# Ten weight low parts and five h low parts per FFN move from GpSimd to VectorE, and ScalarE's queue is reordered around them

## The chip, the cores and the metric

The kernel runs on one core of a Trainium2 chip. The metric is the device time of one execution in microseconds. Five engines work side by side, each on its own queue of instructions in program order: TensorE (PE, matmul), VectorE (DVE), ScalarE (ACT), GpSimd (POOL) and SyncE (SP), which issues the DMA transfers. They meet only at semaphores.

## The reference, cut to what matters

Two layers of a decoder trunk, on 544 token columns (512 of a prompt and 32 of samples). Each layer has three residual updates, of which the first and the third are FFNs, and the change touches only them. So there are four FFNs in the program:

```python
def swiglu(x, w_gate, w_up, w_down):
    return (jax.nn.silu(x @ w_gate) * (x @ w_up)) @ w_down

x = x + 0.5 * rmsnorm(swiglu(rmsnorm(x, g[0]), ffn1_w_gate, ffn1_w_up, ffn1_w_down), g[1])
# then the token mixer, then the same with ffn2_* and g[4], g[5]
```

D_MODEL is 1024 (8 chunks of 128) and D_FF 2688 (21 tiles of 128). h = silu(gate) * up is a tensor of 21 tiles of 128 x 544. All values are float32.

## The kernel before, in words

**High and low parts.** The matmuls take operands rounded to a shorter float format (fp32r). To keep the accuracy of float32, each operand is split: `hi` is the rounded value, and `lo = value - hi`. A product of two operands is three matmuls: w_hi with x_hi, w_hi with x_lo, w_lo with x_hi (`pe_step`, L995). ScalarE makes the high parts (`act_high`, L1619 to 1626, a Copy into fp32r), and another engine the low parts by a subtraction.

**Weight blocks.** A block is 128 x 512, four chunks of one weight column tile, so a gate or an up tile takes two blocks. Blocks pass through three rings: `w_raw` with 3 slots (the DMA's target), `w_hi` and `w_lo` with 6 slots each. SyncE may load block n once block n-3 has its low part (`w_split`, L588). ScalarE may make the high part of item n once TensorE has used item n-6 (L1625).

**The up stage of an FFN.** Tiles 0 to 5 (PLAIN_TILES = 6) are plain: 6 gate and 6 up tiles make 12 units of two blocks, blocks 0 to 23. The first three units are done in the opening (`pe_opening`), interleaved with the end of the sublayer before; units 3 to 11 follow in the loop of L1118. Even units are gate tiles, odd units up tiles, and unit i writes the PSUM pair i % 3, so it must wait until VectorE has read unit i-3 from there: an even unit waits for the `up` of two tiles before (`up_read`, L1123), an odd unit for the `gate` of the tile before (`gate_scaled`, L1125). Unit 9, for one, waits for gate(3). Each block also waits for its low part (L1101). The tiles 6 to 20 are then computed as 15 pair steps of seven products each (`pe_product`), with mixed operands that VectorE and ScalarE prepare during units 3 to 11: `x_mix(c)` and `x_lows(c)` for c = 0 to 3 on VectorE, `act_x_operands(c)` on ScalarE. Product `MIXED2`, the third of a step, waits until ScalarE has copied the first product out (`z_kept`, L1149), and for that copy ScalarE waits at the first step for the low part of h tile 4 (L1868).

**Who does what there.** VectorE: `gate(t)` (one operation), `up(t)` (two), `x_mix(c)` (five), `x_lows(c)` (four), then `w_mix` and `w_lower` for the pair steps, in the order of L2488 to 2515. ScalarE: `silu(t)`, `h_high(t)` (the high part of h tile t), `high(i)` and `act_x_operands(c)`, in the order of L1889 to 1919. GpSimd: the low part of every plain weight block (`split`, L877 to 883, the instruction is L882) and of every h tile (`low(t)`, L894 to 898), in the order of L900 to 912. gate(t) for t from 3 on overwrites a buffer that holds h tile t-3, and so waits for that tile's low part (L2377).

The order of all this is written out by hand; there is no planner. SyncE issues the loads in the order of L609 to 643, with the stores of x to a scratch tensor (`x_aside`) and the loads for pair step 0 between the block loads.

Of the kernel before, what the change touches and what calls it, by code (L numbers as in the profile page):

```python
# [18 lines left out]
def program(nc, I, O):  # L19
# [28 lines left out]

    PLAIN_TILES = 6
    LENT_TILES = 4  # L50
    PAIRS = FC - PLAIN_TILES
    UP_PLAIN = 4 * PLAIN_TILES
    PRODUCTS = 7
# [37 lines left out]
    def split_by(n):  # L91

        return plain(n) + 1
# [57 lines left out]
    with ExitStack() as ctx:  # L151
# [166 lines left out]
        def h_tile(t):  # L318

            if t < EARLY_H:  # L320
                return h_hi[:, t, :], h_lo[:, t, :]
            return xn_hi[:, t - EARLY_H, :], xn_lo[:, t - EARLY_H, :]
# [549 lines left out]
        def pool_layer(pool, l, steps):  # L872
# [12 lines left out]
            def splits(i0, i1):  # L885
                for i in range(i0, i1):
                    split(i)

            def up(which):

                f0 = FC * (2 * l + which)
                n_up = (B_UP1, B_UP2)[which]

                def low(t):  # L894
                    hi, lo = h_tile(t)
                    buf = t % 3 if t < PLAIN_TILES else (t - PLAIN_TILES) % 2
                    pool.wait_ge(h_hi_ready, f0 + t + 1)
                    pool.tensor_tensor(lo, gs[:, buf, :], hi.bitcast(F32), ALU.subtract).then_inc(h_ready, 1)  # L898

                splits(n_up, n_up + 14)  # L900
                low(0)
                low(1)
                splits(n_up + 14, n_up + 17)
                low(2)
                splits(n_up + 17, n_up + 21)
                low(3)
                splits(n_up + 21, n_up + UP_PLAIN)
                low(4)
                for t in range(PLAIN_TILES - 1, FC - 1):
                    low(t)  # L910
                splits(n_up + UP_ITEMS, n_up + UP_ITEMS + RING)
                low(FC - 1)

# [729 lines left out]
            act.wait_ge(w_used, n - RING + 1)  # L1643
            act.activation(w_hi[:, n % RING, :], w_sum(w, k, plain(n_up + UP_ITEMS)), ACT.Copy).then_inc(w_hi_ready, 1)

        def act_x_operands(act, l, which, c):

            done = 2 * l + which
            b = c % 2
            act.wait_ge(x_normed, 8 * done + 2 * c + 2)  # L1650
            act.activation(x_first[:, c, 0:HT], stage[:, b, 0, :], ACT.Copy).then_inc(x_op_hi, 1)
            act.activation(x_ops[:, 0:2, c, 0:HT], stage[:, b, 2:4, :], ACT.Copy).then_inc(x_op_hi, 1)
            act.wait_ge(x_mixed, 12 * done + 3 * c + 1)
            act.activation(x_ops[:, 2:4, c, 0:HT], x_ops_f[:, 2:4, c, HT:T], ACT.Copy).then_inc(x_op_hi, 1)
            act.wait_ge(x_mixed, 12 * done + 3 * c + 3)
            act.activation(x_r[:, c:DC:4, 0:HT], x[:, c:DC:4, half(1)], ACT.Copy).then_inc(x_op_hi, 1)
# [165 lines left out]
        def act_ffn(act, l, which):  # L1822

            v = 3 * l + 2 * which
            f0 = FC * (2 * l + which)
            n_up = l * BLOCKS + (B_UP1, B_UP2)[which]
            n_dn = l * BLOCKS + (B_DN1, B_DN2)[which]
            g0 = PLAIN_TILES * (2 * l + which)
            pairs0 = PAIRS * (2 * l + which)

            def silu(t):
                act.wait_ge(gate_scaled, g0 + t + 1)
                act.activation(gs[:, t % 3, :], gs[:, t % 3, :], ACT.Silu).then_inc(silu_done, 1)

            def h_high(t):
                if which == 1 and t == 0:
                    act.wait_ge(cs_stored, 16 * HC * (l + 1))
                act.wait_ge(h_scaled, f0 + t + 1)
                buf = t % 3 if t < PLAIN_TILES else (t - PLAIN_TILES) % 2
                act.activation(h_tile(t)[0], gs[:, buf, :], ACT.Copy).then_inc(h_hi_ready, 1)  # L1840

            def high(i):
                if i < UP_PLAIN:
                    act_high(act, n_up + i)
                elif i < UP_ITEMS:
                    act_high_of_pair(act, l, which, *divmod(i - UP_PLAIN, PRODUCTS))
                else:
                    act_high(act, n_dn + i - UP_ITEMS)

            def second_silu(w):  # L1850
                act.wait_ge(w_used, n_up + UP_PLAIN + PRODUCTS * w + A22 + 1)
                act.activation(gs[:, w % 2, half(1)], ps[:, ZS[w % 2], 0:HT], ACT.Silu).then_inc(silu_kept, 1)

            def pair_step(w):

                n = n_up + UP_PLAIN + PRODUCTS * w
                i = UP_PLAIN + PRODUCTS * w
                mixed = (rstd[:], gs[:, 2, :])[w % 2]
                z = ps[:, ZS[w % 2], 0:HT]

                def keep(k, out, src):
                    act.wait_ge(w_used, n + k + 1)
                    act.activation(out, src, ACT.Copy).then_inc(z_kept, 1)  # L1863

                if w:
                    second_silu(w - 1)
                high(i + 5)
                act.wait_ge(h_ready, f0 + PLAIN_TILES + w - 1)  # L1868
                keep(A11, gs[:, w % 2, half(0)], z)
                high(i + 6)  # L1870
                h_high(PLAIN_TILES + w - 1)
                if w:
                    act.wait_ge(second_summed, 2 * (pairs0 + w) - 1)
                keep(A22MINUS21, p_kept[:], ps[:, SECOND_COLS[w % 2], 0:HT])
                high(i + 7)
                if w == 0:
                    act.wait_ge(h_scaled, f0 + PLAIN_TILES)
                elif w == 1:
                    act.wait_ge(h_ready, f0 + PLAIN_TILES)
                keep(MIXED2, mixed[:, half(0)], z)  # L1880
                high(i + 8)
                high(i + 9)
                keep(A11MINUS21, mixed[:, half(1)], z)
                act.wait_ge(first_summed, pairs0 + w + 1)
                act.activation(gs[:, w % 2, half(0)], gs[:, w % 2, half(0)], ACT.Silu).then_inc(silu_kept, 1)
                high(i + 10)
                high(i + 11)

            act_open(act, v, n_up, [gs[:, 0, :], gs[:, 2, :], gs[:, 1, :]])  # L1889
            silu(0)  # L1890
            silu(1)
            act_x_operands(act, l, which, 0)
            h_high(0)
            h_high(1)
            high(14)
            silu(2)
            high(15)
            act_x_operands(act, l, which, 1)
            high(16)
            h_high(2)  # L1900
            high(17)
            act_x_operands(act, l, which, 2)
            high(18)
            silu(3)
            high(19)
            high(20)
            h_high(3)
            high(21)
            act_x_operands(act, l, which, 3)
            high(22)  # L1910
            silu(4)
            high(23)
            high(24)
            h_high(4)
            high(25)
            high(26)
            silu(5)
            high(27)
            high(28)
            for w in range(PAIRS):  # L1920
                pair_step(w)
            second_silu(PAIRS - 1)
            high(UP_ITEMS + 5)
            h_high(FC - 1)
            act.preload_act_table_set("natural_log_exp_and_others")
            for t in range(DC - 1):
                for b in range(DOWN_BLOCKS):
                    act_high(act, n_dn + DOWN_BLOCKS * (t + 1) + b)
                act_square(act, v, t)
            act_turn_from_ffn(act, v, n_dn + DOWN_BLOCKS * DC)  # L1930
# [422 lines left out]
        def dve_ffn(dve, l, which):  # L2353
# [94 lines left out]
            def w_mix_second(w, n, slot, mixed0):  # L2448
# [8 lines left out]
                dve.wait_ge(w_mixed, mixed0 + 3)  # L2457
                dve.tensor_tensor(slot[6], slot[2], slot[3], ALU.add).then_inc(w_mixed, 1)

            def w_lower(w, k):  # L2460
                n = n_up + UP_PLAIN + PRODUCTS * w + k
                slot = w_slot(w, k, after)
                dve.wait_ge(w_hi_ready, n + 1)
                dve.tensor_tensor(slot, w_sum(w, k, after), w_hi[:, n % RING, :].bitcast(F32), ALU.subtract).then_inc(w_low, 1)  # L2464
# [24 lines left out]
            gate(0)  # L2489
            gate(1)  # L2490
            x_mix(0)
            up(0)
            up(1)
            x_lows(0)
            gate(2)
            x_mix(1)
            up(2)
            x_lows(1)
            x_mix(2)
            gate(3)  # L2500
            x_lows(2)
            up(3)
            x_mix(3)
            gate(4)
            x_lows(3)
            w_mix(0, (0,))
            up(4)
            w_mix(0, (1,))
            w_lower(0, 0)
            w_lower(0, 1)  # L2510
            w_lower(0, 2)
            gate(5)
            w_lower(0, 3)
            w_lower(0, 4)
# [592 lines left out]
```

## Time and profile before

| | us |
|---|---|
| median of 3 runs | 2137.16 |
| lowest and highest | 2136.04, 2138.46 |
| the profiled execution | 2134.72 |
| its span in the trace | 2133.0 |
| TensorE busy in the span | 2096.6 (98%) |
| VectorE busy | 1343.7 (63%) |
| ScalarE busy | 1000.9 (47%) |
| GpSimd busy | 789.9 (37%) |

Read the waits of TensorE first, then the stretch in which they lie, engine by engine. In a timeline a row is one instruction or a run of equal ones: start, duration, engine, line of the kernel, what it writes and reads, how many, and in brackets how long the engine stood idle before it and who ended that. A matmul's duration is modelled and overlaps the next one's, so the pitch of matmuls is read from the starts.

### The profile page before, as it was taken

Reading aid. Unit: us, or ns where it says so; the run is one execution under the profiler, and the core shown is the slowest. Engines: PE = TensorE matmul, PEld = TensorE weight load, DVE = VectorE, ACT = ScalarE, POOL = GpSimd, SP = SyncE. Lnnn points to the kernel's source line nnn. Section 1 sums busy time; section 2 is a strip of 40 time slices with the busy share of each in tenths; the row PEclk is TensorE's granted clock in tenths of the full one; section 3 lists DMA queues with packets and bytes.
Section 4 is the critical chain, followed back from the end, with each engine's and each line's share of the span. In section 5 each row is a group of like instructions: output and inputs, shape, how many; then the busy total and the mean of one; then the engine's idle time right before and its main releaser. Section 6 shows DMA issues by size and latency. Waiting matters only on the chain.

```text
span 2133.0 us, 45510 instructions
## 1 busy us (share of the span) xinstructions
PE 2096.6 (98%) x18864; PEld 2044.2 (96%) x18864; DVE 1343.7 (63%) x2147; ACT 1000.9 (47%) x2031; POOL 789.9 (37%) x645
## 2 busy tenths in 40 slices
PE   8999999999999999999999999999999999999999
PEld 8899999999889989999999999999998899999998
DVE  6999611666457899950189994036554678999313
ACT  5466522534344646652265664235143545566422
POOL 4411374533324431134443113544332354311442
PEclk9999999999999999999999999999999999999999
DMA  5333442322233423343242334333224134233432
GB/s 174 89 100 100 128 110 84 91 71 66 61 93 103 127 85 100 102 128 97 80 138 84 103 100 140 94 89 81 72 61 101 57 114 128 86 103 101 129 90 78
DMA packets 395245, 209.79 MB, mean 98 GB/s; under 512 B 31920, under 2 KB 385472, under 8 KB 395040
## 3 DMA queue, kind: packets, MB, share of 16 engines
q1 hardware_dynamic: 394896, 206.84, 34.3%
q8 instruction: 149, 2.44, 0.5%
q14 instruction: 56, 0.46, 0.1%
q10 hardware_dynamic: 144, 0.06, 0.0%
HBM read 189.18 MB, written 17.67 MB: 97 GB/s over the span
## 4 chain that ended last, share of the span: by engine, by line
PE 83%; DVE 12%; ACT 2%; issue 1%; DMA 1%; POOL 1%; SPq 0%; DVEq 0%; ACTq 0%
PE ps L1001 47%; PE ps L1013 28%; PE ps L1284 1%; DVE x_ops L2420 1%; DVE stage L2399 1%; DVE xn_lo L2222 1%; DVE x_ops L2417 1%; DVE x_ops_f L2402 1%; POOL w_lo L882 1%; DMA w_raw<-in_ffn_w_up 1%; DVE numer L2846 1%; DVE x_r L2422 1%; DVE x L2238 1%; DVE spare L2464 1%; DVE x_first L2415 1%
## 5 line engine op out<-in xcount | busy, mean ns | idle before, releaser
L882 POOL TENSOR_TENSOR w_lo<-w_raw,w_hi 128x512 fp32r<-128x512 f32 (+1 forms) x440 | 578.6, 1325 | 769.2 <-ACT w_hi L1626 767.7
L1001 PE MATMUL ps<-xn_hi,w_hi 128*128 128x272 f32 x2496 | 572.0, 296 | 17.8 <-POOL w_lo L882 13.3
L1001 PE MATMUL ps<-xn_hi,w_lo 128*128 128x272 f32 x2496 | 555.3, 289 | 0.0
L1001 PE MATMUL ps<-xn_lo,w_hi 128*128 128x272 f32 x2496 | 554.2, 289 | 0.0
L1626 ACT ACTIVATE w_hi<-w_raw 128x512 fp32r<-128x512 f32 (+1 forms) x440 | 264.6, 605 | 597.2 <-PE ps L1001 463.0
L1001 PEld LDWEIGHTS ps<-xn_hi,w_hi 128*128 128x128 f32 x2496 | 408.1, 190 | 40.1 <-issue 30.8
L1001 PEld LDWEIGHTS ps<-xn_lo,w_hi 128*128 128x128 f32 x2496 | 409.0, 190 | 0.3
L1001 PEld LDWEIGHTS ps<-xn_hi,w_lo 128*128 128x128 f32 x2496 | 407.1, 190 | 0.0
L1013 PE MATMUL ps<-x_ops,w_hi 128*128 128x272 f32 x1920 | 368.8, 289 | 0.3
L1013 PEld LDWEIGHTS ps<-x_ops,w_hi 128*128 128x128 f32 x1920 | 302.1, 189 | 1.6 <-ACT rstd L1863 1.1
L2204 DVE TENSOR_TENSOR acc<-acc,gs 128x544 f32<-128x544 f32 (+1 forms) x45 | 35.2, 781 | 319.9 <-ACT gs L1696 319.3
L898 POOL TENSOR_TENSOR h_lo<-gs,h_hi 128x544 fp32r<-128x544 f32 x52 | 90.2, 1737 | 299.9 <-ACT h_hi L1840 299.9
L1013 PE MATMUL ps<-x_r,w_hi 128*128 128x272 f32 x960 | 185.6, 288 | 2.2 <-ACT gs L1863 2.2
L1001 PE MATMUL ps<-h_hi,w_hi 128*128 128x272 f32 x832 | 181.1, 289 | 0.0
L1001 PE MATMUL ps<-h_lo,w_hi 128*128 128x272 f32 x832 | 180.3, 288 | 0.0
L1001 PE MATMUL ps<-h_hi,w_lo 128*128 128x272 f32 x832 | 180.2, 288 | 0.0
L1013 PEld LDWEIGHTS ps<-x_r,w_hi 128*128 128x128 f32 x960 | 151.2, 189 | 2.8 <-ACT gs L1863 2.8
L898 POOL TENSOR_TENSOR xn_lo<-gs,xn_hi 128x544 fp32r<-128x544 f32 x32 | 57.1, 1783 | 243.0 <-ACT xn_hi L1840 243.0
L1001 PEld LDWEIGHTS ps<-h_lo,w_hi 128*128 128x128 f32 x832 | 133.2, 188 | 0.2
L1001 PEld LDWEIGHTS ps<-h_hi,w_hi 128*128 128x128 f32 x832 | 133.1, 188 | 0.2
L1001 PEld LDWEIGHTS ps<-h_hi,w_lo 128*128 128x128 f32 x832 | 132.9, 188 | 0.0
L1013 PE MATMUL ps<-x_ops,w_lo 128*128 128x272 f32 x448 | 129.3, 289 | 0.0
(402 smaller groups left out, 3512.2 us busy)
## 6 DMA issues: line engine op xcount, KB each, us to landing
w_raw<-in_ffn_w_down SPq DMA_DIRECT2D x160, 256.0 KB, 2.8
w_raw<-in_w_in SPq DMA_DIRECT2D x120, 256.0 KB, 2.9
w_raw<-in_ffn_w_gate SPq DMA_DIRECT2D x76, 256.0 KB, 2.9
spare_f<-in_ffn_w_gate SPq DMA_DIRECT2D x64, 256.0 KB, 2.8
spare_f<-in_ffn_w_up SPq DMA_DIRECT2D x64, 256.0 KB, 2.9
w_lo_f<-in_ffn_w_up SPq DMA_DIRECT2D x56, 256.0 KB, 2.9
w_raw<-in_ffn_w_up SPq DMA_DIRECT2D x48, 256.0 KB, 2.9
x_aside<-x SPq DMA_DIRECT2D x16, 544.0 KB, 4.5
```

What stands on the lines that cost most here:

```text
L882: pool.tensor_tensor(w_lo[:, q % RING, 0:m], w_raw[:, q % RAW, 0:m], w_hi[:, n % RING, 0:m].bitcast(F32), ALU.subtract).then_inc(w_split, 1)
L898: pool.tensor_tensor(lo, gs[:, buf, :], hi.bitcast(F32), ALU.subtract).then_inc(h_ready, 1)
L1001: mm = pe.matmul(pair(p)[:, a, :], w, z[:, half(a)], start=(k == 0 and j == 0), stop=(k == chunks - 1 and j == 2))
L1013: mm = pe.matmul(ps[:, bank, 0:HT], w, z, start=(first and c == 0 and j == 0), stop=(c == 3 and j == 2), skip_group_check=not first)
L1284: mm = pe.matmul(ps[B * j:B * j + n, 4 + hh, at:at + w], proj[rows_, k0 + kt, ts], q, start=True, stop=True)
L1626: act.activation(w_hi[:, n % RING, 0:m], w_raw[:, q % RAW, 0:m], ACT.Copy).then_inc(w_hi_ready, 1)
L2204: dve.tensor_tensor(acc[:, w], gs[:, 0, w] if t == 1 else acc[:, w], gs[:, t % 3, w], ALU.add).then_inc(y_summed, 1)
L2222: dve.scalar_tensor_tensor(xn_lo[:, k, half(a)], x[:, k, half(a)], gain(l, 2 * s, k), xn_hi[:, k, half(a)].bitcast(F32), ALU.mult, ALU.sub ...
L2238: dve.tensor_tensor(xk, xk, y[:, k - 1, half(a)], ALU.add).then_inc(x_updated, 1)
L2399: dve.scalar_tensor_tensor(stage[:, b, 2 * j:2 * j + 2, :], halves(x[:, c + 4 * j, :]), gain(l, 4 * which, c + 4 * j), pair(3), ALU.mult, ...
L2402: dve.tensor_tensor(x_ops_f[:, 2:4, c, HT:T], stage[:, b, 0:4:3, :], stage[:, b, 1:2, :].broadcast_to([P, 2, HT]), ALU.subtract).then_inc( ...
L2415: dve.tensor_tensor(x_first[:, c, HT:T], stage[:, b, 0, :], x_first[:, c, 0:HT].bitcast(F32), ALU.subtract).then_inc(x_op_ready, 1)
```

## The change

VectorE makes the low parts of the plain weight blocks 14 to 23 and of h tiles 0 to 4 in each FFN; GpSimd keeps blocks 0 to 13 and h tiles 5 to 20. On GpSimd's queue two waits stand in place of the moved work. `act_x_operands` is cut in two, `act_x_plain` (x_first and the first two of x_ops) and `act_x_mixed` (the last two and x_r), and the high parts 14 to 28 stand at other places of ScalarE's queue. On VectorE's queue x_lows(2) now comes before gate(3), x_mix(3) before up(3), x_lows(3) before gate(4), and up(4) behind both halves of w_mix(0) and w_lower(0, 0).

```diff
+    POOL_SPLITS = 14
@@ GpSimd, up(which)
-                splits(n_up, n_up + 14)
-                low(0)
-                low(1)
-                splits(n_up + 14, n_up + 17)
-                low(2)
-                splits(n_up + 17, n_up + 21)
-                low(3)
-                splits(n_up + 21, n_up + UP_PLAIN)
-                low(4)
+                splits(n_up, n_up + POOL_SPLITS)
+                pool.wait_ge(h_ready, f0 + PLAIN_TILES - 1)
                 for t in range(PLAIN_TILES - 1, FC - 1):
                     low(t)
+                pool.wait_ge(w_split, split_by(n0 + n_up + UP_PLAIN - 1))
                 splits(n_up + UP_ITEMS, n_up + UP_ITEMS + RING)
@@ ScalarE, act_ffn, the new order in full
+            silu(0) high(14) silu(1) act_x_plain(0) high(15) act_x_mixed(0) high(16)
+            h_high(0) h_high(1) high(17) silu(2) act_x_plain(1) high(18) act_x_mixed(1)
+            h_high(2) high(19) act_x_plain(2) high(20) act_x_mixed(2) silu(3) high(21)
+            act_x_plain(3) high(22) act_x_mixed(3) h_high(3) high(23) high(24) silu(4)
+            high(25) h_high(4) high(26) high(27) silu(5) high(28)
@@ VectorE, dve_ffn
+            def w_split_here(i):
+                n = n_up + i
+                q = plain(n)
+                if i == POOL_SPLITS:
+                    dve.wait_ge(w_split, q)
+                dve.wait_ge(w_hi_ready, n + 1)
+                dve.tensor_tensor(w_lo[:, q % RING, :], w_raw[:, q % RAW, :], w_hi[:, n % RING, :].bitcast(F32), ALU.subtract
+                                  ).then_inc(w_split, 1)
+
+            def h_low(t):
+                hi, lo = h_tile(t)
+                dve.wait_ge(h_hi_ready, f0 + t + 1)
+                dve.tensor_tensor(lo, gs[:, t % 3, :], hi.bitcast(F32), ALU.subtract).then_inc(h_ready, 1)
@@ VectorE, the order from gate(0) on
             gate(0)
             gate(1)
             x_mix(0)
+            w_split_here(14)
             up(0)
             up(1)
             x_lows(0)
+            w_split_here(15)
             gate(2)
+            h_low(0)
+            h_low(1)
             x_mix(1)
+            w_split_here(16)
             up(2)
             x_lows(1)
+            w_split_here(17)
             x_mix(2)
+            h_low(2)
+            w_split_here(18)
+            x_lows(2)
+            w_split_here(19)
             gate(3)
-            x_lows(2)
+            x_mix(3)
+            w_split_here(20)
             up(3)
-            x_mix(3)
+            x_lows(3)
+            w_split_here(21)
+            h_low(3)
+            w_split_here(22)
             gate(4)
-            x_lows(3)
+            w_split_here(23)
             w_mix(0, (0,))
-            up(4)
             w_mix(0, (1,))
             w_lower(0, 0)
+            up(4)
             w_lower(0, 1)
             w_lower(0, 2)
+            h_low(4)
             gate(5)
```

## Rows read from the trace of the kernel before

**Rows 1.** Whom TensorE waited for, whole program: us, times, longest.
```profile
PE ps L1001 <- POOL w_lo L882: 13.3, 4, 4.0
```

**Rows 2.** Timeline of TensorE at the start of unit 9, in the four FFNs.
```profile
73.51 0.49 PE L1001 MATMUL ps<-xn_hi,w_hi 128*128 128x272 f32 x2 [2.57 <-POOL w_lo L882]
...
756.98 0.41 PE L1001 MATMUL ps<-xn_lo,w_hi 128*128 128x272 f32 x2
757.23 0.41 PE L1001 MATMUL ps<-xn_hi,w_lo 128*128 128x272 f32 x2
761.60 0.49 PE L1001 MATMUL ps<-xn_hi,w_hi 128*128 128x272 f32 x2 [3.96 <-POOL w_lo L882]
...
1127.71 0.79 PE L1001 MATMUL ps<-xn_hi,w_hi 128*128 128x272 f32 x2 [3.33 <-POOL w_lo L882]
...
1815.05 0.79 PE L1001 MATMUL ps<-xn_hi,w_hi 128*128 128x272 f32 x2 [3.43 <-POOL w_lo L882]
```

**Rows 3.** Timeline of TensorE at the third product of pair step 0, two FFNs.
```profile
785.00 0.52 PE L1013 MATMUL ps<-x_r,w_hi 128*128 128x272 f32 x2 [0.60 <-ACT gs L1863]
...
1838.59 0.42 PE L1013 MATMUL ps<-x_r,w_hi 128*128 128x272 f32 x2
```

**Rows 4.** Timeline of VectorE in the second FFN's units 3 to 9.
```profile
729.25 1.35 DVE L2369 TENSOR_TENSOR gs<-gs,ps 128x544 f32<-128x544 f32 x2 [5.51 <-ACT ps L1686]
...
735.52 0.72 DVE L2384 TENSOR_TENSOR gs<-gs 128x544 f32<-128x544 f32 x1
...
738.30 1.20 DVE L2415 TENSOR_TENSOR x_first<-stage,x_first 128x272 fp32r<-128x272 f32 x1
...
755.46 1.46 DVE L2399 SCALAR_TENSOR_TENSOR stage<-x,par,ps 128x544 f32<-128x544 f32 x2
...
758.63 0.71 DVE L2378 TENSOR_TENSOR gs<-ps,rstd 128x544 f32<-128x544 f32 x1
759.26 0.43 DVE L2415 TENSOR_TENSOR x_first<-stage,x_first 128x272 fp32r<-128x272 f32 x1
...
760.24 1.79 DVE L2420 TENSOR_TENSOR x_ops<-x_ops_f,x_ops 128x544 fp32r<-128x544 f32 x1
```

**Rows 5.** Timeline of GpSimd, second FFN: the splits of blocks 18 to 20.
```profile
759.99 4.90 POOL L882 TENSOR_TENSOR w_lo<-w_raw,w_hi 128x512 fp32r<-128x512 f32 x3 [5.68 <-ACT w_hi L1626]
```

**Rows 6.** Instructions on tile x_ops, VectorE's two low parts, all FFNs: ns min/median/max.
```profile
L2417 DVE TENSOR_TENSOR x_ops<-stage,x_ops x16: 715/1272/1885, 51.4 to 1824.1; 128x544 fp32r<-128x544 f32 x16
L2420 DVE TENSOR_TENSOR x_ops<-x_ops_f,x_ops x16: 1787/1806/1875, 53.2 to 1824.8; 128x544 fp32r<-128x544 f32 x16
```

**Rows 7.** Timeline of VectorE: two subtractions of a weight high part, back to back.
```profile
791.23 0.68 DVE L2464 TENSOR_TENSOR w_raw_r<-w_raw,w_hi 128x512 fp32r<-128x512 f32 x1
791.83 0.69 DVE L2464 TENSOR_TENSOR w_lo<-w_lo_f,w_hi 128x512 fp32r<-128x512 f32 x1
```

**Rows 8.** Timeline of VectorE: gate(0) and up(0) in the first and the third FFN.
```profile
42.80 1.35 DVE L2369 TENSOR_TENSOR gs<-gs,ps 128x544 f32<-128x544 f32 x2 [0.64 <-ACT ps L1686]
...
47.54 0.72 DVE L2384 TENSOR_TENSOR gs<-gs 128x544 f32<-128x544 f32 x1
...
1095.96 1.35 DVE L2369 TENSOR_TENSOR gs<-gs,ps 128x544 f32<-128x544 f32 x2 [4.93 <-ACT ps L1686]
...
1101.30 0.72 DVE L2384 TENSOR_TENSOR gs<-gs 128x544 f32<-128x544 f32 x1
```

**Rows 9.** ScalarE's high parts (717 to 773 us), then the load of block 16 alone.
```profile
L1626 ACT ACTIVATE w_hi<-w_raw x18: 612/618/635, 716.9 to 771.5; 128x512 fp32r<-128x512 f32 x18
...
w_raw<-in_ffn_w_gate SPq DMA_DIRECT2D x1, 256.0 KB, 4.1
```

**Rows 10.** Timeline of SyncE: block 16 is issued (second FFN).
```profile
734.85 0.37 SPq L589 DMA_DIRECT2D w_raw<-in_ffn_w_gate  x1
```

**Rows 11.** Stretches of 1 us: busy by engine, TensorE's granted clock, DMA share, GB/s.
```profile
763.00:764.00 1.00, 1.00 (x6) 1.00 (x6) 1.00 (x2) 0.00 (x0) 1.00 (x2) 0.50 0.74 214
...
1814.00:1815.00 1.00, 0.00 (x0) 0.00 (x0) 1.00 (x1) 0.95 (x2) 1.00 (x2) 0.50 0.00 0
```

More of the change, by code:

```diff
@@ L1644, in act_high_of_pair, with act_x_plain @@
             act.activation(w_hi[:, n % RING, :], w_sum(w, k, plain(n_up + UP_ITEMS)), ACT.Copy).then_inc(w_hi_ready, 1)
-        def act_x_operands(act, l, which, c):
+        def act_x_plain(act, l, which, c):
             done = 2 * l + which
@@ L1652, in act_x_operands, with act_x_mixed @@
             act.activation(x_ops[:, 0:2, c, 0:HT], stage[:, b, 2:4, :], ACT.Copy).then_inc(x_op_hi, 1)
+        def act_x_mixed(act, l, which, c):
+            done = 2 * l + which
             act.wait_ge(x_mixed, 12 * done + 3 * c + 1)
@@ L1890, in act_ffn @@
             silu(0)
+            high(14)
             silu(1)
-            act_x_operands(act, l, which, 0)
+            act_x_plain(act, l, which, 0)
+            high(15)
+            act_x_mixed(act, l, which, 0)
+            high(16)
             h_high(0)
             h_high(1)
-            high(14)
+            high(17)
             silu(2)
-            high(15)
-            act_x_operands(act, l, which, 1)
-            high(16)
+            act_x_plain(act, l, which, 1)
+            high(18)
+            act_x_mixed(act, l, which, 1)
             h_high(2)
-            high(17)
-            act_x_operands(act, l, which, 2)
-            high(18)
+            high(19)
+            act_x_plain(act, l, which, 2)
+            high(20)
+            act_x_mixed(act, l, which, 2)
             silu(3)
-            high(19)
-            high(20)
+            high(21)
+            act_x_plain(act, l, which, 3)
+            high(22)
+            act_x_mixed(act, l, which, 3)
             h_high(3)
[L1908 to L1911, printed above, removed]
             high(23)
             high(24)
+            silu(4)
+            high(25)
             h_high(4)
-            high(25)
             high(26)
+            high(27)
             silu(5)
-            high(27)
             high(28)
```

## The prediction

> **What bounds the kernel now.** The table of engine shares comes first: TensorE is busy for nearly the whole span, so only what makes TensorE wait, or run slow, can be worth anything. The waits of TensorE come next. Its largest entry is the low part of a weight block made by GpSimd, 13.3 us in 4 waits [rows 1]. The timeline shows that they are one wait in each FFN, always at the same place, the first matmul of unit 9 (block 18): 2.57, 3.96, 3.33 and 3.43 us [rows 2]. I count a loss from the moment the next matmul would have started. Matmul pairs start 0.25 apart, so unit 9 could have started at 757.48 in the second FFN and did at 761.60, a loss of 4.12, which is the idle time plus 0.16 [rows 2]. The four losses are 2.73, 4.12, 3.49 and 3.59, together 13.9.
>
> The stage loses more behind it. From unit 9 to the third product of the first pair step lie 3 x 48 + 24 = 168 matmuls, 21.1 us at 0.125 each. It took 785.00 - 761.60 = 23.40 in the second FFN and 23.54 in the fourth [rows 2, 3] (the first and third are within 0.01 of the second). That is 2.3 lost three times and 2.44 once, 9.3 together. Part of it is TensorE's clock, at 0.50 of full speed for some us behind the wait in the second to fourth FFN [rows 11], but the first FFN, with no such stretch, loses the same 2.3: the third product waits for a copy by ScalarE [rows 3], whose operands come off VectorE's chain. So VectorE's chain sets both ends. In all 23.2 us lie here.
>
> What sets VectorE's chain is GpSimd. In the second FFN GpSimd's split of block 18 starts at 759.99 [rows 5], VectorE's x_ops low part starts at 760.24 and takes 1.79 [rows 4], and the same shape takes 0.715 at its fastest [rows 6]. 760.24 + 1.79 - 0.72 = 761.31, when the first of GpSimd's three splits is about over: the operation seems to stand until GpSimd is done. GpSimd in turn takes 4.90 for three splits [rows 5].
>
> **The change, part by part.** I lay out VectorE's queue for the second FFN from 735.52, the start of up(0) [rows 4]. Until there nothing moves: gate(0), gate(1) and x_mix(0) stand as before, beside GpSimd's blocks 12 and 13. From there GpSimd has nothing until h tile 5, so I take durations from rows with GpSimd idle, start to start.
> - Added up to gate(3): splits 14 to 19, six at 791.83 - 791.23 = 0.60 [rows 7], 3.60. Three h low parts at 0.64 (the x_ops shape has the same elements: 0.715 less the overlap of 0.08 that the weight rows show), 1.92.
> - Kept: three up at (738.30 - 735.52) / 2 = 1.39, 4.17. Two x_mix at 758.63 - 755.46 = 3.17, 6.34. Three x_lows: the first two operations took 760.24 - 759.26 = 0.98, the other two I put at 0.64 each, so 2.26 and 6.78. gate(2) 0.63 and gate(3) 0.71 to its end, 1.34 [rows 4].
> - Sum 24.15: gate(3) ends at 759.67. Before, it ended at 758.63 + 0.71 = 759.34 [rows 4]. The relief from GpSimd pays for nine added operations but for 0.3 us.
>
> Split 18 ends about 3.6 us ahead of gate(3) (x_lows(2) 2.26, split 19 0.60, gate 0.71), at 756.1, before unit 9 could want it at 757.48. So the wait on the low part goes, and what is late next is gate(3), which frees unit 9's PSUM pair. It was hidden behind the split before and is not now. TensorE starts 761.60 - 761.31 = 0.29 behind a release, so at 759.96: a loss of 2.48 in place of 4.12.
>
> The other FFNs differ in how long gate(0) to up(0) takes: 4.74 in the first, 5.34 in the third (the fourth has the third's within 0.01), 6.27 in the second [rows 4, 8]. First: 47.54 + 24.15 + 0.29 = 71.98 against 73.51 - 2.73 = 70.78, a loss of 1.20. Third: 1125.74 against 1124.22, 1.52. Fourth: 1.6 likewise. New losses at unit 9: 6.8 in place of 13.9.
>
> Behind unit 9 VectorE has 18.1 us of TensorE's work as cover. From gate(3): x_mix(3) 3.17, split 20 at 763.4 (wanted at 766.0), up(3) read at 764.1 (the same), x_lows(3), split 21 at 767.7 (wanted 769.0, the tightest, 1.3 to spare), h_low(3), split 22, gate(4) at 769.6 (wanted 772.0), split 23, four w_mix, w_lower(0, 0) at 773.2 (wanted 778.1), up(4), w_lower(0, 1) and (0, 2), h_low(4) at about 777.2. ScalarE's first copy waits for that last one, and is wanted when the first product ends at 779.6. So the 9.3 behind unit 9 goes too, if the clock stays up. A later gate(3) moves TensorE's wants along with it, so these margins hold in all four.
>
> ScalarE: no operation is added; 15 high parts, four silu and the x operands stand in another order. high(14) to high(17) stand before the h high parts that VectorE wants. The first risk is that a block has not landed: block 16 is issued at 734.85, now as before, and takes 4.1 [rows 10, 9], so ScalarE stands at high(16) till 738.95, and h_high(0) behind it, some 0.6 each [rows 9], ends at 740.2; VectorE wants it at 742.4. I cost the order at nothing; that 2.2 is the cover, and each us beyond it would move gate(3) by one. high(20) is the other such place, with h_high(3) far behind it.
>
> SyncE: the load of block n+3 goes when block n has its low part. Split 14 is done at 736.2, and every load from block 17 on goes some us earlier, with the pair loads that stand between them. With 4.1 to land there is no block that VectorE waits for. GpSimd: its two new waits have only h tile 5 and the down blocks behind them, whose operands come later than both.
>
> Gain: 23.2 - 6.8 = 16.4 us. The profiled execution took 2134.7 (span 2133.0 and 1.7 around it), so it would be 2118.3; the median shown is 2.4 above it, 2137.2, and I put the same on the forecast: **2121**.
>
> The unproven price in this is L2420, the third operation of x_lows. It took 1.79 or more in all 16 instances [rows 6]; I put it at 0.72 because L2417, of the same shape and type, does so with GpSimd idle. The bounds are 0.72 and 1.8. I take the lower since in the instance of [rows 4, 5] its end fits GpSimd's end.
>
> The Trainium skill speaks to this on the page "SBUF — State Buffer", section "Who interferes with whom": a VectorE instruction with two SBUF inputs contends with a GpSimd instruction that reads SBUF, and whoever is second is blocked for the whole instruction of the other. By that rule the 16 slow instances are an accident of when GpSimd starts, and gate(3) ends at 759.7; by the row of L2420 read alone, three of them keep 1.1 more each, and it ends at 762.9.
>
> **The rivals.**
> - *VectorE's slow durations are its own.* The place is the same chain. Before, 735.52 to 759.34 took 23.8 for operations that I price at 18.6 without the additions: 5.2 per FFN is to vanish. If none did, gate(3) would be late by 5.2 more in each, losses at unit 9 of 6.8 + 20.8, and idle times over 6 us with the clock at half behind each, 1.7 x 4 (six matmuls in a us in place of ten or so, over 3.4 us as in the second FFN [rows 11]). 34.4 in place of 23.2: 2148. It decides from 16.4 / 4 = 4.1 us per FFN on (less with the clock). L2420 alone, 3.3 per FFN and the clock, gives 2120.7 + 13.1 + 6.8 = 2140.6. For it: 16 of 16. Against it: [rows 4, 5].
> - *The clock falls all the same.* I count on idle times of about 2.3, 1.0, 1.4 and 1.4. An idle of 2.57 left it up in the first FFN [rows 2], but in the fourth it was at 0.50 from 1814 on, with the engine idle since 1811.62 and the restart at 1815.05 [rows 2, 11], so it fell within some 2.4 us of idle. With no wait left behind unit 9 to hide it, it costs its full 1.7 in each, most likely in the second FFN. All four: 2127.5; one: 2122.5.
> - *ScalarE's order stalls VectorE.* A block that lands late at high(14), high(16) or high(18) blocks silu or h_high. The first 2.2 us are free at the place worked out; a stall of 4 beyond them per FFN would leave no change, 2137. For it: the load of block 16 shares the queues with the last store of x and took 4.1, and one such that took 2.2 longer would be felt. Against it: by block 17 the stores of x are over.
> - *gate(3) is no wait.* If x_mix runs quicker than I took it, up to 23.2 goes: 2114.
>
> **How the numbers follow.** Forecast 0.66 (with the clock falling once, 2119 to 2124), clock in most FFNs 0.14, stalls of ScalarE's order 0.09 (2127 to 2138), VectorE's own durations 0.07 (2135 to 2148), no wait at all 0.04. About 0.2%, 4.3 us, is what a measurement here can tell from no change. Slower by that, over 2141.4, is most of the case of VectorE's own durations and a little of the one of ScalarE's order: 0.06. Within it, 2132.9 to 2141.4: 0.08. Faster: 0.86. The range, 2114 to 2131, has the first two cases, the last, and half of the stalls.
>
> **What would show it.** In the trace after: TensorE's wait on L882 at unit 9 is gone, and in its place stands a wait of 1 to 2.4 us on VectorE's gate (L2378, at its new line); x_ops low parts of 0.72 on units 3 to 9; GpSimd idle between block 13 and h tile 5; no wait of TensorE in the first pair step; GpSimd less busy by some 60 operations of 1.3 to 1.6 us, 80 to 95 us. Wrong would be: L2420 at 1.8 with GpSimd idle; a wait on VectorE's split or on a `w_hi` of ScalarE; slow clock behind all four waits.

## The result, and the profile after

| | before | after |
|---|---|---|
| median on this chip, us (lowest to highest) | 2137.81 (2136.04 to 2139.61, 4 runs) | 2122.7 (2120.19 to 2125.51, 4 runs) |
| ratio | | 0.993, 95% interval 0.9912 to 0.9947 |
| the profiled execution, its span | 2134.72, 2133.0 | 2120.19, 2118.5 |
| GpSimd busy | 789.9 | 693.4 |

The change is faster by 15 us, 0.7%, over three times what a measurement here can tell from no change. First, as before, whom TensorE waited for (us, times, longest). Left out is a wait of 4.8 for the load of the norm gains at the start of the program, which was 5.0 before; these are the next two:

```profile
PE ps L996 <- DVE gs L2381: 4.7, 4, 1.8
PE ps L996 <- DVE xn_lo L2225: 4.0, 5, 2.3
```

The wait of [rows 1] is gone. In its place stands one for gate(t) (L2381). The timeline of TensorE shows it at the same four places, the starts of unit 9, which answer to [rows 2]. Behind it stands the start of the first pair product (x_first) in each FFN, and for the second FFN that of x_r, which answers to [rows 3]:

```profile
72.49 0.52 PE L996 MATMUL ps<-xn_hi,w_hi 128*128 128x272 f32 x2 [0.79 <-DVE gs L2381]
...
90.65 0.41 PE L1008 MATMUL ps<-x_first,w_hi 128*128 128x272 f32 x2
...
755.91 0.52 PE L996 MATMUL ps<-xn_hi,w_hi 128*128 128x272 f32 x2 [0.79 <-DVE gs L2381]
...
774.08 0.41 PE L1008 MATMUL ps<-x_first,w_hi 128*128 128x272 f32 x2
...
777.09 0.42 PE L1008 MATMUL ps<-x_r,w_hi 128*128 128x272 f32 x2
...
1118.00 0.52 PE L996 MATMUL ps<-xn_hi,w_hi 128*128 128x272 f32 x2 [1.35 <-DVE gs L2381]
...
1136.14 0.41 PE L1008 MATMUL ps<-x_first,w_hi 128*128 128x272 f32 x2
...
1800.86 0.52 PE L996 MATMUL ps<-xn_hi,w_hi 128*128 128x272 f32 x2 [1.80 <-DVE gs L2381]
...
1820.54 0.41 PE L1008 MATMUL ps<-x_first,w_hi 128*128 128x272 f32 x2
```

Unit 9 to x_r took 777.09 - 755.91 = 21.18 us, where it took 23.40 before [rows 2, 3] and where 168 matmuls need 21.1: nothing is lost behind unit 9 any more. From unit 9 to x_first it is 18.16, 18.17, 18.14 and, in the fourth, 19.68. The stretches of 1 us in the fourth (busy by engine, granted clock, DMA share, GB/s) say why:

```profile
1801.00:1802.00 1.00, 1.00 (x6) 1.00 (x7) 1.00 (x2) 1.00 (x2) 0.00 (x0) 0.67 0.47 135
1802.00:1803.00 1.00, 1.00 (x7) 1.00 (x6) 0.91 (x2) 0.80 (x3) 0.00 (x0) 0.50 0.43 128
1803.00:1804.00 1.00, 1.00 (x6) 1.00 (x6) 0.91 (x3) 1.00 (x3) 0.00 (x0) 0.50 0.00 0
1804.00:1805.00 1.00, 1.00 (x7) 1.00 (x6) 1.00 (x2) 0.81 (x2) 0.00 (x0) 0.63 0.00 0
```

The granted clock falls to 0.50, which is 1.2 of 2.4 GHz, behind an idle time of 1.80. The counts in brackets take in instructions that only overlap a stretch; how fast the matmuls go is read from the starts, and there pairs are 0.45 apart in place of 0.25:

```profile
1802.03 0.66 PE L996 MATMUL ps<-xn_hi,w_hi 128*128 128x272 f32 x2
1802.48 0.66 PE L996 MATMUL ps<-xn_lo,w_hi 128*128 128x272 f32 x2
```

That took 19.68 - 18.15 = 1.5 us.

VectorE's timeline in the second FFN answers to [rows 4]. "Low part n" is that of weight block n, the prediction's split n. The rows are low part 14, up(0), the x_ops low part that never took less than 1.79 before, low part 18, for which unit 9 waited before, and gate(3).

```profile
731.71 0.68 DVE L2469 TENSOR_TENSOR w_lo<-w_raw,w_hi 128x512 fp32r<-128x512 f32 x1
732.31 0.72 DVE L2387 TENSOR_TENSOR gs<-gs 128x544 f32<-128x544 f32 x1
...
736.08 0.72 DVE L2423 TENSOR_TENSOR x_ops<-x_ops_f,x_ops 128x544 fp32r<-128x544 f32 x1
...
751.69 0.68 DVE L2469 TENSOR_TENSOR w_lo<-w_raw,w_hi 128x512 fp32r<-128x512 f32 x1
...
755.15 0.71 DVE L2381 TENSOR_TENSOR gs<-ps,rstd 128x544 f32<-128x544 f32 x1
```

Low part 18 is done at 752.37, 3.5 us ahead of unit 9's start. From low part 14 to the end of gate(3) it is 755.86 - 731.71 = 24.15 us. All 16 instances of each x_ops low part are now alike (ns, min/median/max), where [rows 6] had medians of 1272 and 1806:

```profile
L2420 DVE TENSOR_TENSOR x_ops<-stage,x_ops x16: 715/718/719, 52.0 to 1806.2; 128x544 fp32r<-128x544 f32 x16
L2423 DVE TENSOR_TENSOR x_ops<-x_ops_f,x_ops x16: 714/717/724, 52.7 to 1806.9; 128x544 fp32r<-128x544 f32 x16
```

From gate(0) to the end of gate(3) VectorE took 28.46, 30.09, 29.49 and 29.51 us in the four FFNs before, and takes 28.92, 29.37, 29.66 and 29.71 now. In that time it does thirteen operations more: the nine moved ones, and the four of x_lows(2), which stood behind gate(3) before. The relief from GpSimd pays for them, and low part 18, which came behind gate(3) before, now comes 3.5 us ahead of it.

### The profile page after: what moved, and what is told of

It reads as the page before. It is cut to its first block, busy times and chain, and to the rows that moved or that the text cites. A ratio compares the mean times of both kernels' runs of the same rounds, so it can differ in the third digit from the quotient of the medians.

```text
span 2118.5 us, 45522 instructions
## 1 busy us (share of the span) xinstructions
PE 2092.5 (99%) x18864; PEld 2041.5 (96%) x18864; DVE 1324.3 (63%) x2207; ACT 1004.9 (47%) x2031; POOL 693.4 (33%) x585
## 4 chain that ended last, share of the span: by engine, by line
PE 86%; DVE 10%; ACT 1%; issue 1%; DMA 1%; POOL 0%; SPq 0%; DVEq 0%; ACTq 0%
PE ps L996 49%; PE ps L1008 30%; PE ps L1279 1%; DVE xn_lo L2225 1%; DVE stage L2402 1%; DVE w_lo L2469 1%; DVE numer L2878 1%; DVE x L2241 1%; DMA w_raw<-in_ffn_w_up 0%; DVE x_ops_f L2405 0%; DVE y_ffn L2237 0%; POOL w_lo L883 0%; PE ps L1531 0%; DVE x_r L2425 0%; DVE h_lo L2475 0%
## 5 line engine op out<-in xcount | busy, mean ns | idle before, releaser
L883 POOL TENSOR_TENSOR w_lo<-w_raw,w_hi 128x512 fp32r<-128x512 f32 (+1 forms) x400 | 514.0, 1294 | 716.0 <-ACT w_hi L1621 714.5
L996 PEld LDWEIGHTS ps<-xn_hi,w_hi 128*128 128x128 f32 x2496 | 406.9, 189 | 32.6 <-issue 16.3
L899 POOL TENSOR_TENSOR h_lo<-gs,h_hi 128x544 fp32r<-128x544 f32 x32 | 58.6, 1832 | 432.5 <-ACT h_hi L1839 432.5
```

The costliest lines, as they stand in the source:

```text
L883: pool.tensor_tensor(w_lo[:, q % RING, 0:m], w_raw[:, q % RAW, 0:m], w_hi[:, n % RING, 0:m].bitcast(F32), ALU.subtract).then_inc(w_split, 1)
L996: mm = pe.matmul(pair(p)[:, a, :], w, z[:, half(a)], start=(k == 0 and j == 0), stop=(k == chunks - 1 and j == 2))
```

## The experiments

Times are medians in us, each with its ratio to the kernel before beside it on the same chip and the 95% interval. That one had 2137.72 (19 runs) for ScalarE's order, the weight parts, the h parts and gate(3) earlier; 2137.97 (9 runs) for the additions, the fills, low part 21 and the change again; 2136.5 (9 runs) for the last two.

**ScalarE's new order alone.** The kernel before, with nothing but ScalarE's queue as in the change.

```diff
             silu(0)
             high(14)
-            silu(1) act_x_operands(0) h_high(0) h_high(1) ...
+            silu(1) act_x_plain(0) high(15) act_x_mixed(0) high(16) h_high(0) h_high(1) ...
```

> Before with ScalarE's new order alone; VectorE and GpSimd work and are ordered as before. Theory A (VectorE's chain, stretched by GpSimd's reads beside it, sets both ends): gate(3) and the third product of the first pair step stay where they were, 2134 to 2138; TensorE's wait at unit 9 moves from the split of block 18 to gate(3), about 2 us shorter, and comes back behind it. Theory B (ScalarE's old order, with the high parts behind the x operands, made the low parts late): at least half of the gain, 2124 to 2130.

Measured: 2137.66, ratio 1.0006 (0.9997 to 1.0015). No gain and no loss, but the waits of TensorE are others than in [rows 1, 2]:

```profile
PE ps L1002 <- POOL w_lo L883: 13.1, 8, 2.5
PE ps L1002 <- DVE gs L2387: 4.4, 4, 1.1
```

Here unit 9 waits 1.10 to 1.13 for gate(3), and in each FFN block 21 waits 2.5 for GpSimd, whose queue has the low part of h tile 3 ahead of it. The order moves the waits; the chain of VectorE and GpSimd sets the end all the same. So the order is worth nothing by itself. It may be needed by the rest all the same: before, GpSimd stood idle 5.68 us for ScalarE's high part 18 ahead of its low part [rows 5]. The moved work with ScalarE's old order was not run, so what the order adds to it is not shown.

**The ten weight low parts alone.** The changed kernel, with the h low parts back on GpSimd.

```diff
-                pool.wait_ge(h_ready, f0 + PLAIN_TILES - 1)
-                for t in range(PLAIN_TILES - 1, FC - 1):
+                for t in range(FC - 1):
                     low(t)
@@ VectorE
-            h_low(0) h_low(1) ... h_low(2) ... h_low(3) ... h_low(4)
```

> The change with the h low parts left on GpSimd. VectorE loses three operations of 0.64 ahead of gate(3) and gets three GpSimd operations beside it, each of which can hold one of its own for up to 1.3. Theory A: about as the change or up to 2 us per FFN worse, 2122 to 2130. Theory B: as the change, 2121 to 2124.

**The h low parts alone.** The changed kernel, with blocks 14 to 23 back on GpSimd.

```diff
-                splits(n_up, n_up + POOL_SPLITS)
+                splits(n_up, n_up + UP_PLAIN)
@@ VectorE
-            w_split_here(14) ... w_split_here(23)
```

> The change with the ten low parts of blocks 14 to 23 left on GpSimd, ScalarE in the new order. VectorE loses six operations of 0.60 ahead of gate(3) and has six GpSimd operations beside it. In the trace before, nine of these stretched the chain by 5.2, 0.58 each, so gate(3) would stand about where it stands in the change. Theory A: 2122 to 2132, with x_ops low parts of up to 1.8 again. Theory B: as the change, 2121 to 2124.

Measured: 2129.47 (0.9966, 0.9954 to 0.9978) and 2129.21 (0.9962, 0.9951 to 0.9974). Each brings about half, and the sum, 8.3 + 8.5 = 16.8, is within what both together brought on three occasions, 15.1, 17.8 and 12.6. TensorE's wait for gates is the one that grew, nearly all of it at unit 9 for gate(3), first with the weight parts moved alone, then with the h parts alone:

```profile
PE ps L995 <- DVE gs L2380: 13.7, 5, 4.6
```
```profile
PE ps L995 <- DVE gs L2380: 9.6, 4, 4.3
```

The timelines of the second kernel (h parts alone) show the mechanism in two instances. VectorE and, below, GpSimd:

```profile
751.83 1.82 DVE L2424 TENSOR_TENSOR x_r<-x,x_r 128x544 fp32r<-128x544 f32 x1
...
756.75 1.82 DVE L2474 TENSOR_TENSOR h_lo<-gs,h_hi 128x544 fp32r<-128x544 f32 x1
...
759.48 0.72 DVE L2422 TENSOR_TENSOR x_ops<-x_ops_f,x_ops 128x544 fp32r<-128x544 f32 x1
```
```profile
751.58 1.48 POOL L883 TENSOR_TENSOR w_lo<-w_raw,w_hi 128x512 fp32r<-128x512 f32 x1 [1.52 <-ACT w_hi L1620]
...
756.65 1.34 POOL L883 TENSOR_TENSOR w_lo<-w_raw,w_hi 128x512 fp32r<-128x512 f32 x1 [3.58 <-ACT w_hi L1620]
```

Both operations that start beside a GpSimd low part here, x_r and an h part, take 1.8; the x_ops part, 1.8 in all 16 instances before, takes 0.72 with GpSimd idle. It is not the line that is slow, it is the company.

One expectation missed: with the h parts alone gate(3) was to stand about where it stands in the change. From gate(0) to its end it took 30.76, 30.27, 32.01 and 29.02, against 28.92, 29.37, 29.66 and 29.71, so later in three FFNs, by up to 2.35. That rested on 0.58 for each GpSimd operation, 5.2 us over nine. In the second FFN before, from up(0) to gate(3), GpSimd's timeline has seven (h tiles 0 to 2, weight blocks 14 to 17), and seven VectorE instructions beside them took 7.4 us more than in the change, 1.06 for each.

**GpSimd reads beside VectorE again.** The changed kernel, with eight additions on GpSimd that nothing uses.

```diff
                 splits(n_up, n_up + POOL_SPLITS)
+                for _ in range(8):
+                    steps[0] += 1
+                    pool.tensor_tensor(idle_f[:, 0:4 * P]..., ones[:]..., ident[:]..., ALU.add).then_inc(const_ready, 1)
+                    pool.wait_ge(const_ready, steps[0])
```

> The changed kernel, and in each FFN eight more GpSimd additions of 128x512 float32 with two operands in SBUF, put right behind its fourteen low parts; nothing uses what they write, so the kernel's own work is unchanged. VectorE's queue, its operands and its order are those of the change. Theory: what slowed VectorE's chain before was GpSimd reading SBUF beside it, not how much VectorE had to do. Then the two-operand instructions of VectorE beside these eight grow again, the x_ops addition towards the 1.79 to 1.88 us that it took before, the chain from low part 14 to the end of gate(3) grows from 24.15 us by 4 to 9 us in each FFN, unit 9 starts that much later, and the time is 2136 to 2155. Rival: the chain became short because the queue is ordered another way; GpSimd beside it costs nothing, the x_ops addition stays at 0.72, and the time is that of the change, 2120 to 2124.

**GpSimd writes beside VectorE.** The same place, sixteen fills.

```diff
+                for _ in range(16):
+                    steps[0] += 1
+                    pool.memset(idle_f[:, 0:4 * P], 0.0).then_inc(const_ready, 1)
+                    pool.wait_ge(const_ready, steps[0])
```

> The changed kernel, and at the same place in each FFN sixteen GpSimd fills of 128x512 float32, which write SBUF and read none of it; nothing uses them. Theory: only GpSimd's reads stand in the way of VectorE's second operand, so the x_ops addition stays at 0.72 us, gate(3) ends where it does in the change, and the time is 2120 to 2124. Rival: any work of GpSimd in SBUF slows VectorE; then the x_ops addition is near 1.8 us where a fill is beside it, and the time is above 2130. The Trainium skill (SBUF — State Buffer, section Who interferes with whom) states the first: a VectorE instruction with two SBUF inputs contends with a GpSimd instruction that reads SBUF, not with one that only writes it.

Measured: 2151.87 (1.0068, 1.0054 to 1.0082) with the additions, 2121.67 (0.9927, 0.9914 to 0.9939) with the fills. The timelines of the second FFN, first with the additions (GpSimd, then VectorE beside it), then with the fills:

```profile
737.68 12.66 POOL L905 TENSOR_TENSOR idle_f<-ones,ident 128x512 f32<-128x512 f32 x8
```
```profile
741.14 1.78 DVE L2474 TENSOR_TENSOR w_lo<-w_raw,w_hi 128x512 fp32r<-128x512 f32 x1
742.85 1.81 DVE L2392 TENSOR_TENSOR gs<-gs 128x544 f32<-128x544 f32 x1
744.69 0.72 DVE L2397 TENSOR_TENSOR gs<-gs,ps 128x544 f32<-128x544 f32 x1
...
749.12 1.80 DVE L2428 TENSOR_TENSOR x_ops<-x_ops_f,x_ops 128x544 fp32r<-128x544 f32 x1
750.84 0.71 DVE L2430 TENSOR_TENSOR x_r<-x,x_r 128x544 fp32r<-128x544 f32 x1
```
```profile
729.66 9.32 POOL L905 MEMSET idle_f<- 128x512 f32 x16
```
```profile
731.86 0.72 DVE L2392 TENSOR_TENSOR gs<-gs 128x544 f32<-128x544 f32 x1
...
735.62 0.71 DVE L2428 TENSOR_TENSOR x_ops<-x_ops_f,x_ops 128x544 fp32r<-128x544 f32 x1
```

The additions run from 737.68 to 750.34. Every VectorE instruction that starts in that time with both inputs in SBUF is slower than in the change, and the three from 744.69 on, with one input in PSUM, are not. As soon as GpSimd is done, x_r takes 0.71. With sixteen fills beside it VectorE's chain is what it is in the change, 755.39 - 731.25 = 24.14 us from low part 14 to the end of gate(3). So it is GpSimd's reads, not its presence, and not VectorE's order of work. The description of the kernel says that the engines meet only at semaphores; these two runs show that VectorE and GpSimd also meet where they read SBUF. The Trainium skill says the same on the page "SBUF — State Buffer", section "Who interferes with whom", and these two runs agree with it on both halves, reads and writes.

The price, from x_mix(0) to low part 15: 751.48 - 735.29 = 16.19 us with the additions, 737.35 - 727.76 = 9.59 in the change. Low part 14 to the end of gate(3) takes 769.97 - 741.14 = 28.83, 4.7 more than 24.15; the whole stretch under the additions lost 6.6 for eight of them, 0.83 each (from gate(0) to the end of gate(3) it is 6.6 in all four FFNs), to an engine that does such an operation itself in 0.60 to 0.64. TensorE then waits for gates 28.0 us in all:

```profile
PE ps L1001 <- DVE gs L2386: 22.7, 8, 4.6
PE ps L1001 <- DVE gs L2395: 5.3, 4, 1.7
```

That is 23.3 more than in the change. Unit 9 to x_first takes 20.12, 19.68, 20.33 and 19.65, each behind an idle time of 4.63 to 4.64 and at granted clock 0.50; over 18.15 each it is 7.2, where the change has 1.5. Together 29.0, of the 30.7 us between the spans, 2149.2 and 2118.5.

**gate(3) earlier.** The changed kernel, with the gate that unit 9 waits for ahead of x_lows(2), behind low part 18.

```diff
             w_split_here(18)
+            gate(3)
             x_lows(2)
             w_split_here(19)
-            gate(3)
             x_mix(3)
```

> The change with gate(3) ahead of x_lows(2) and split 19 on VectorE. If gate(3) is the only thing that holds unit 9 after the change: it ends 2.9 us earlier, the four waits (0.8, 0.8, 1.35, 1.8 idle and 0.16 each) go, and the slow clock in the fourth FFN (1.6). Split 21 is then wanted some 1 to 2 us earlier against VectorE's chain and may cost up to 1 us in the third and fourth. 2115 to 2119. Rival: another wait stands right behind, 2121 to 2124.

**The same, and low part 21 earlier too.**

```diff
             up(3)
+            w_split_here(21)
             x_lows(3)
-            w_split_here(21)
-            h_low(3)
             w_split_here(22)
             gate(4)
+            h_low(3)
             w_split_here(23)
```

> The changed kernel with gate(3) right behind low part 18 and ahead of x_lows(2), as in the run before, and besides low part 21 ahead of x_lows(3), which is held behind it, and h_low(3) behind gate(4). Only one wait of TensorE was left behind unit 9 in the run before, 0.35 us for a low part in the fourth FFN. Theory: nothing on VectorE is late any more, so this takes 0.3 us at most, 2117 to 2119. Rival: h_low(3) or x_lows(3) now comes late at its own product and gives it back, 2119 to 2122, with a new wait of TensorE for VectorE behind unit 10.

**The change again,** for a comparison on the same chip.

> The changed kernel as it is, beside the three others on one chip, so that they are compared with it directly. 2119 to 2125, as it was; the mixer of the first layer shows whether its lower clock of the first profile is there again: if it is in every profile of the change, it belongs to the change and takes 1 to 3 us of the gain, else it is scatter.

Measured: 2118.62 (0.9913, 0.99 to 0.9926) for gate(3) earlier; 2119.61 (0.9916, 0.9903 to 0.993) with low part 21 as well; 2120.14 (0.9922, 0.9909 to 0.9936) for the change. With gate(3) earlier TensorE waits nowhere in these units for VectorE but once:

```profile
PE ps L996 <- DVE w_lo L2469: 0.3, 1, 0.3
```

Low part 21 earlier takes that wait away and puts two others in its place, for up(3) and for ScalarE's copy:

```profile
PE ps L996 <- DVE gs L2390: 1.4, 2, 1.0
PE ps L1008 <- ACT gs L1862: 1.1, 2, 0.5
```

It is no gain; its rival, that the time is given back, has the profile on its side. The change again has the lower clock in the first mixer once more, 0.83 over 530 to 540, so by what was expected it goes with the change and is not scatter; the run with the fills, which lacks it, speaks against that. From 2119.61 and 2120.14, four runs each, nothing can be told of gate(3), so it ran once more beside the change.

**gate(3) earlier and the change, side by side.**

> The changed kernel with gate(3) right behind low part 18 once more, now beside the changed kernel itself on one chip. Its first trace had 0.3 us of TensorE waits on VectorE at units 9 and 10 where the change has 4.7 to 5.0, and its median was 2118.6 where the change had 2120.1 and 2122.7 on other occasions. Theory: the waits are saved in full, and its median is 3 to 5 us under that of the change on this chip. Rival: what it saves is given back at places where TensorE waits for other things, or lies inside the scatter of 2 to 5 us between executions, and the two medians are less than 2 us apart.

> The changed kernel as it is, for the comparison with the run before on one chip: 2119 to 2124, with 4.5 to 5.2 us of TensorE waits for gate(3) at unit 9 in its trace.

Measured: 2118.93 (0.9916, 0.9903 to 0.993) against 2123.91 (0.9947, 0.9933 to 0.996), 5.0 us apart, with intervals that do not overlap. The profiles say less: in this execution with gate(3) earlier TensorE still waited 1.9 us for VectorE (1.0 and 3 times 0.3), and in that of the change 3.9, yet its span is the longer one, 2119.1 against 2117.7: of the runs each had, the profiled one was the slowest with gate(3) earlier and the fastest of the change. Over both occasions gate(3) earlier has medians of 2118.6 and 2118.9, the change 2122.7, 2120.1 and 2123.9. The change's 3.9 is under the 4.5 to 5.2 expected. I take gate(3) earlier as some 3 us faster than the change, an estimate from these medians; the waits saved in the traces are 2.0 here and 4.4 on the first occasion. By the medians it beats both kernels, and low part 21 earlier can't be told from it.

## Why the prediction was right

Forecast 2121.0, measured 2122.7 (2120.1 and 2123.9 on other occasions), and in the profiled execution 2120.19 for 2118.3.

*GpSimd's reads stretch VectorE's chain; with them gone the chain is 24.15 us.* Right to the digit, 24.15 in the second FFN, and the same in the first. The unproven price, 0.72 for L2420, held in all 16. The rival that the durations are VectorE's own is dead: the runs with parts moved show the same line slow or fast by what GpSimd does, and the one with eight additions brings it back. The rule from the Trainium skill (page "SBUF — State Buffer", section "Who interferes with whom"), which gave 759.7 against 762.9, was the better guide than 16 equal rows. One sum beside it was wrong, though no part of the forecast: before, 23.8 us were set against a price of 18.6, which has three x_lows in it, while x_lows(2) stood behind gate(3) then [rows 4]. Without it the price is 16.4, so GpSimd stretched the chain by 7.4 us and not by 5.2. The rival was priced too low by 2.2 per FFN, and 24.15 pays for thirteen operations and not for nine.

*gate(3) is late next, and unit 9 loses 1.20, 2.48, 1.52 and 1.6.* The kind was right, and the new wait stands where it was to stand. As idle plus 0.16 it measured 0.95, 0.95, 1.51 and 1.96, 5.4 in place of 6.8. The second FFN was the term most off. I let nothing move ahead of up(0), but gate(0) to up(0) took 732.31 - 726.49 = 5.82 with low part 14 in it, so 5.22 without, and not 6.27: GpSimd's blocks 12 and 13 slowed one of x_mix(0)'s instructions (1.51) where they had slowed two (1.66 and 1.34). With ScalarE's order alone the same stretch took 5.33, so the 6.27 was the value of one profile and no fixed term. That is 1.05 of the 1.53. The release is 0.24 of it: I took 0.29 from GpSimd's end to TensorE's start, and from VectorE's gate(3) it is 755.91 - 755.86 = 0.05. The 0.29 was too long already before: I had worked out that GpSimd's low part 18 ended at 761.31, and the trace has it from 759.99 to 761.45, 0.15 ahead of TensorE. And TensorE itself, counted from gate(0), wants unit 9 0.24 later than before (754.96 - 726.49 = 28.47; 757.48 - 729.25 = 28.23).

Of the four idle times, 0.79, 0.79, 1.35 and 1.80, two lie under the 1 to 2.4 that was named as the sign.

*The clock.* The likeliest case had one fall, worth 1.7, from a count of six matmuls in a us for ten; by the starts they are 0.45 a pair for 0.25. One fall came, worth 1.5, but in the fourth FFN, behind the longest idle time; I had named the second. In the change's second profile, with 1.74 idle at the same place, unit 9 to x_first was 18.16 and none came. The losses with it are 5.4 + 1.5 = 6.9. The sum had 6.8 at unit 9 and nothing for the clock, so two errors of 1.4 and 1.5 cancel, and that is luck.

*The 9.3 behind unit 9 goes.* Right: 21.18 for 21.1, and no wait of TensorE in the first pair step.

*ScalarE's order costs nothing.* Right. High part 16 waited for its block until 735.09, 0.77 idle, and there was one of 0.97 at high part 19; neither reached VectorE. By itself the order brings nothing (1.0006).

*Gain 16.4.* Losses fell from 23.2 to 6.9, by 16.3, and the span by 14.5. Two places gave some back. At the start of the program the first sums ahead of gate(0) began at 40.54 and not 39.78, 0.76 later. In the mixer of the first layer the clock fell while TensorE was busy all the time, which the prediction had nowhere (two rows of 2 us):

```profile
530.00:532.00 2.00, 2.00 (x22) 1.91 (x23) 0.14 (x1) 0.96 (x5) 1.04 (x1) 0.89 0.01 4
532.00:534.00 2.00, 2.00 (x11) 2.00 (x10) 0.03 (x1) 0.00 (x0) 0.00 (x0) 0.50 0.50 131
```

It costs about 1.5: the same matmul began at 507.4 where it was 510.9 before, 3.5 earlier, and one behind the fall at 538.7 for 540.7, 2.0 earlier. 16.3 - 0.8 - 1.5 leaves 14.0 of the 14.5.

*GpSimd's share.* 96.5 us less, where I had 80 to 95: its instructions had been stretched as well.

## What to carry to other kernels

A GpSimd instruction that reads SBUF beside a VectorE chain of two-operand work is paid for by VectorE, 0.83 us each with the additions and 1.06 each in the second FFN before. If VectorE does it itself in 0.60 to 0.64, an engine that is 63% busy overall but sets the end of a stage gets faster by taking on more. The kernel with gate(3) earlier shows it with the same queue: ahead of gate(3) VectorE has what it had before and eight operations more, and from gate(0) to the end of gate(3) it takes 26.06 to 26.91 us where it took 28.46 to 30.09. Look for it where one line shows 0.72 and 1.8 us for the same shape, and lay GpSimd's rows beside it before calling the line slow. Then place the instruction that frees the next buffer (here gate(3)) directly behind the last thing that is needed sooner.

## What was not expected of the hardware

- GpSimd suffers too: eight additions took 12.66 us beside VectorE, 1.58 each, where the shortest of all 32 took 1.29 and its low parts of the same size take 1.28 to 1.30 alone. It loses 0.3 each, VectorE 0.83.
- VectorE's release of gate(3) reaches TensorE in 0.05 us. GpSimd's of low part 18 took 0.15 before (0.14 in the first FFN), and its release of block 21 took 0.05 in the run with ScalarE's order alone (from 772.02 to 772.07), so the difference does not belong to the engine.
- The clock fall in the first mixer, at 0.83 over 530 to 540, is in all three profiles of the change and in four others (h parts alone, gate(3) earlier twice, low part 21 earlier), and in none of before, ScalarE's order alone, weight parts alone, the additions and the fills. TensorE had been busy without a wait. The kernel with the fills is the changed kernel in this stage and lacks it, and it has the shortest span but one, 2115.7. What sets it was not found; it shows that 1.5 us of a profile's span can come from a stage whose code the change leaves alone.
